# Expert gate weights: one-hot products on TensorE replaced by 384 adding indirect DMAs into a zeroed DRAM table, and 40 tiles of gelu results kept on chip

## What is computed

```
sc = scores of 8 heads x 2 halves against 128 keys each
s_top, i_top = top_k(sc, 16)                       # per half
best, pos = top_k(all 16 x 16 sums, 16)            # per head
idx = i_top[half 0] * 128 + i_top[half 1]          # 16384 experts
g = softmax(best)
out = sum over 8 heads x 16 ranks of  g * gelu(u_tab[idx] . x) * v_tab[idx]
```

## Time and profile before

| | |
|---|---|
| median of 3 runs | 2199.63 us (2199.42 to 2200.46) |
| span of the profiled execution | 2200.7 us, so about 1 us over the median |
| PE, DVE, ACT, POOL busy | 95%, 77%, 38%, 35% of the span |
| DMA, mean over the span | 195 GB/s |
| u stage | 1087 to 1662 us of the span |
| v stage | 1662 to 2187 us of the span |

### The profile page before, as it was taken

The page is one execution under the profiler, slowest core; times in us unless marked ns, Lnnn a source line. Parts: engine busy times, 40 slices in busy tenths (PEclk is TensorE's granted clock), DMA queues, the critical chain, the costliest instruction groups (busy, mean ns, idle before and its releaser), DMA issues.

```text
span 2200.7 us, 35703 instructions
## 1 busy us (share of the span) xinstructions
PE 2099.8 (95%) x11175; PEld 1853.1 (84%) x11175; DVE 1692.5 (77%) x3372; ACT 828.2 (38%) x1439; POOL 773.6 (35%) x672
## 2 busy tenths in 40 slices
PE   6998988979999998999899999999999999999997
PEld 4886788758888877899899999999998888888886
DVE  3776555677778744999688888888877888888887
ACT  4454423522323224244444444444433333333333
POOL 2000044500000000334478988988743222222221
PEclk9999989989999999999999999999999999999999
DMA  6743100405234224124477988988789999999995
GB/s 136 94 59 39 20 1 20 133 14 138 69 96 111 79 82 158 58 80 142 165 245 255 320 292 285 315 284 298 256 297 343 342 335 339 338 338 338 336 340 197
DMA packets 229811, 428.46 MB, mean 195 GB/s; under 512 B 18500, under 2 KB 155876, under 8 KB 229476
## 3 DMA queue, kind: packets, MB, share of 16 engines
q1 hardware_dynamic: 173108, 255.96, 38.5%
q0 software_dynamic: 41472, 151.01, 19.9%
q10 hardware_dynamic: 15152, 20.51, 2.6%
HBM read 381.28 MB, written 46.14 MB: 194 GB/s over the span
## 4 chain that ended last, share of the span: by engine, by line
PE 48%; DMA 1%; DVE 1%; POOL 0%; issue 0%; SPq 0%; ACT 0%; DVEq 0%; POOLq 0%
PE bank L2222 22%; PE bank L2205 20%; PE bank L2186 4%; PE bank L2194 2%; DMA v_gg<-weights 1%; DMA acts<-u_weight_lo 0%; POOL row_slot L1957 0%; DVE u_spread L2380 0%; DVE v_residual L2370 0%; POOL u_two L2128 0%; DVE u_lo L2339 0%; DVEq L2051 0%; SPq L2066 0%; ACT u_spread L2471 0%; SPq L2062 0%
## 5 line engine op out<-in xcount | busy, mean ns | idle before, releaser
L2222 PE MATMUL bank<-u_hi,u_one 128*128 128x512 f32 x768 | 299.1, 389 | 1.6 <-DVE u_two L2342 1.5
L2222 PE MATMUL bank<-u_lo,u_one 128*128 128x512 f32 x768 | 298.8, 389 | 0.0
L2222 PE MATMUL bank<-u_hi,u_two 128*128 128x512 f32 x768 | 298.8, 389 | 0.0
L2205 PE MATMUL bank<-xt_hi,u_hi 128*128 128x384 f32 x832 | 287.1, 345 | 0.0
L2205 PE MATMUL bank<-xt_hi,u_lo 128*128 128x384 f32 x832 | 279.0, 335 | 0.0
L2205 PE MATMUL bank<-xt_lo,u_hi 128*128 128x384 f32 x832 | 278.7, 335 | 0.0
L1957 POOL DMA_INDIRECT row_slot<-in_peer_v_dram,row_index x128 | 141.1, 1102 | 388.0 <-DVE row_x L2350 365.3
L2416 ACT ACTIVATE u_hi<-xh 128x1024 fp32r<-128x1024 f32 x128 | 135.9, 1061 | 330.4 <-PE bank L2222 329.8
L2339 DVE TENSOR_TENSOR u_lo<-xh,u_hi 128x1024 fp32r<-128x1024 f32 x128 | 156.8, 1225 | 78.8 <-ACT u_hi L2416 76.0
L1641 POOL TENSOR_TENSOR k_wlo<-q_raw,k_whi 128x2048 fp32r<-128x2048 f32 x4 | 18.7, 4683 | 467.0 <-ACT k_whi L1769 467.0
L2128 POOL TENSOR_TENSOR u_two<-u_match,u_weight_hi 128x512 fp32r<-128x512 f32 x96 | 162.3, 1691 | 50.7 <-DVE u_match L2268 49.7
(11 more groups left out here) (440 smaller groups left out, 4947.2 us busy)
## 6 DMA issues: line engine op xcount, KB each, us to landing
xh<-in_peer_v_dram SPq DMA_DIRECT2D x128, 512.0 KB
xh<-in_peer_u_dram SPq DMA_DIRECT2D x104, 512.0 KB, 4.5
x_raw<-in_w_in_dram SPq DMA_DIRECT2D x56, 512.0 KB, 6.9
v_ga<-acts SPq DMA_DIRECT2D x128, 192.0 KB
acts<-xh ACTq DMA_DIRECT2D x102, 192.0 KB
weights<-u_spread POOLq DMA_DIRECT2D x32, 512.0 KB
v_gg<-weights SPq DMA_DIRECT2D x128, 128.0 KB
p_raw<-in_w_in_dram SPq DMA_DIRECT2D x12, 1024.0 KB, 10.2
```

The source lines that it names most:

```text
L2205: mm = pe.matmul(k.ps[4 + b][:, 0:DENSE], w[b][:, c, :], x[:, c, 0:DENSE], start=(c == 0 and w is uhi and x is hi), stop=(c == DC - 1 and ...
L2222: mm = pe.matmul(k.ps[q][:, :], h[b][:, t * P:(t + 1) * P], w[b][:, f], start=start and h is hhi and w is vhi, stop=stop and h is hlo, ski ...
```

## The change

1. `delta_prepare` also writes the whole gate table (`weights`, 128 x 128 x 384 floats, 25.2 MB) with zeros: POOL clears a tile of 384 columns, SP issues 8 DMAs and waits for them before the stage's barrier.
2. In `choose_experts` the exp of the chosen scores, the softmax and the addresses are made step by step (`make_gates`, called a step later, after the ranks of the next step) instead of once at the end. `turn_chosen` and the copies to `chosen` go.
3. Each gate weight is added to its place in the table by an indirect DMA of POOL's queue with an adding write, 128 words of 4 bytes (one rank of one head for one tile of 128 tokens): 8 x 16 x 3 = 384 of them. 64 are issued in `choose_experts`, between POOL's low parts, the other 320 in the u stage, spread over tiles 1 to 98 of 104, in one queue with the row gathers. A scatter of head h waits for all 16 of head h - 1 for the same token tile.
4. The one-hots, `weigh`, `spread_tokens`, the sums into `u_spread` and the stores of the table go.
5. The gelu results of the last 40 tiles stay on chip (`kept_acts`, 60 KB per partition, in the place of `u_spread`); they are neither stored nor loaded. The weights are loaded for all 384 tokens (192 KB per tile, before 128 KB).
6. In the v stage DVE multiplies gelu by weight in one instruction right ahead of the tile's low parts, no longer one tile ahead. ACT's first `split` comes after the last gelu. DVE's u stage is unrolled, with 128 dots spread over 104 tiles.

```diff
@@ delta_prepare @@
+            @block.sync
+            def _(sp):
+                n = EXPERT_TILES // pieces
+                sp.wait_ge(zero_made, 1)
+                for i in range(pieces):
+                    sp.dma_start(zeroed[i * n:(i + 1) * n].rearrange("c p t -> p c t"), zero[:, :].unsqueeze(1).to_broadcast([P, n, DENSE])
+                                 ).then_inc(zeros_out, 16)
+                sp.wait_ge(zeros_out, 16 * pieces)
@@ choose_experts @@
-                    if e == EARLY - 1:
-                        turn_chosen()
...
-                    if e == EARLY - 6:
-                        act.wait_ge(s["shifted"], after(steps))
-                        act.activation(best[:, :, :, :], best[:, :, :, :], ACT.Exp).then_inc(s["exped"], 1)
+                    if e in exps_at:
+                        exp(exps_at[e])
...
+                scatters = 0
                 for e in range(EARLY):
                     pool.wait_ge(u_copied, after(4 * (e + 1)))
                     pool.tensor_tensor(u_lo[e % 4], u_turn[e % 2], u_hi[e % 4].bitcast(F32), ALU.subtract).then_inc(u_low, 1)
+                    if e == 2:
+                        pool.wait_ge(s["gate_made"], after(1))
+                    while scatters < EARLY_SCATTERS * (e - 1) // (EARLY - 2):
+                        scatter_weight(pool, table, gate, scatters, scattered)
+                        scatters += 1
...
+def scatter_weight(pool, table, gate, nth, scattered):
+    h, t, a = nth // (LAST * TOPK), nth // TOPK % LAST, nth % TOPK
+    r = h * TOPK + a
+    if h:
+        pool.wait_ge(scattered[t], 16 * TOPK * h)
+    pool.indirect_dma_start(table, bass.IndirectOffsetOnAxis(ap=gate["at"][:, t, r:r + 1], axis=0), gate["weight"][:, t, r:r + 1], None,
+                            compute_op=ALU.add).then_inc(scattered[t], 16)
@@ expert_products, POOL @@
-                pool.wait_ge(weight_split, after(3))
-                weigh(0)
-                fetched = SLOTS
-                for i in range(tiles):
-                    if i + 1 < steps:
-                        weigh(i + 1)
...
+                scatters, fetched = EARLY_SCATTERS, SLOTS
+                left = LAST * RANKS - EARLY_SCATTERS
+                for i in range(1, tiles + 1):
+                    while fetched < min(SLOTS + P * i // tiles, P):
                         fetch(fetched)
                         fetched += 1
+                    while scatters < min(EARLY_SCATTERS + left * i // (tiles - MARGIN), LAST * RANKS):
+                        scatter_weight(pool, table, gate, scatters, scattered)
+                        scatters += 1
@@ expert_products, PE @@
                         multiply(n, u)
-                        if c is not None:
-                            spread_tokens(n * PER + u, u % 2)
@@ expert_products, DVE @@
+                for n in range(rounds):
                     for u in range(PER):
                         if ahead(n, u):
                             low(n, u + 1)
+                        while dots < P * (n * PER + u + 1) // tiles:
+                            dot(dots)
+                            dots += 1
@@ expert_products, SP @@
+                for t in range(LAST):
+                    sp.wait_ge(scattered[t], 16 * RANKS)
+                for u in range(PER):
+                    load_weights(0, u)
@@ expert_products, ACT @@
-                        else:
-                            act.wait_ge(spread_ready, after(steps))
-                            split(0, 0)
...
+                with act.Fori(0, out_rounds) as n:
+                    stored(n)
+                with act.Fori(out_rounds, rounds - 1) as n:
+                    kept(n)
+                kept(rounds - 1)
                 act.wait_ge(dot_done, after(P))
                 act.activation(rows["dot"][:, :], rows["dot"][:, :], ACT.Gelu_apprx_tanh).then_inc(acted, 1)
-                for u in range(1, PER):
-                    split(0, u)
-                with act.Fori(1, v_rounds) as n:
+                with act.Fori(0, v_rounds) as n:
                     for u in range(PER):
                         split(n, u)
```

More of the change, by code:

```diff
@@ L1928, in _ @@
[L1928 to L1934, removed]
@@ L2270, in keep @@
-                def keep(c, step):
-                    for m in range(2):
-                        dve.wait_ge(high_kept, after(step * 2 + (m + 1)))
-                        to, parts = places(c, step, m)
-                        dve.tensor_tensor(to, to, parts[:, 1, :, :], ALU.add).then_inc(spread_kept, 1)
-                def dot(n, slot, count):
-                    dve.wait_ge(row_in[slot], count * 16)
-                    dve.scalar_tensor_tensor(out=rows["slots"][slot][:, :], in0=rows["slots"][slot][:, :], scalar=1.0, in1=rows["x"][:, :],
-                                             op0=ALU.mult, op1=ALU.mult, accum_out=rows["dot"][:, bass.ds(n, 1)]).then_inc(dot_done, 1)
@@ L2283, in body @@
-                def body(n, c):
-                    for u in range(PER):
-                        low(n, u + 1)
-                        if c is not None:
-                            step = n * PER + u
-                            dve.wait_ge(spread_ready, after(step))
-                            dve.wait_ge(two_done, after(step * 2 + 2))
-                            onehots(bass.ds(step * TOK_TILE + TOK_TILE, TOK_TILE), (u + 1) % 2)
-                            dot(n * SLOTS + u, u, n + 1)
-                            keep(c, step)
-                    dot(n * SLOTS + PER, PER, n + 1)
@@ L2296, in late_rounds, with dot @@
-                def late_rounds(n):
+                def dot(n):
+                    dve.wait_ge(row_in[n % SLOTS], (n // SLOTS + 1) * 16)
+                    slot = rows["slots"][n % SLOTS]
+                    dve.scalar_tensor_tensor(out=slot[:, :], in0=slot[:, :], scalar=1.0, in1=rows["x"][:, :],
+                                             op0=ALU.mult, op1=ALU.mult, accum_out=rows["dot"][:, n:n + 1]).then_inc(dot_done, 1)
+                low(0, 0)
+                dots = 0
+                for n in range(rounds):
@@ L2402, in high @@
                                        ACT.Copy).then_inc(s["hi_done"][b], 1)
-                def spread_high(c, step):
-                    act.wait_ge(spread_ready, after(step + 1))
-                    for m in range(2):
-                        to, parts = places(c, step, m)
-                        act.activation(to, parts[:, 0, :, :], ACT.Copy).then_inc(high_kept, 1)
                 def split(n, u):
```

344 lines of the change are left out of this document (134 added, 210 removed).

## The result

| | before | after |
|---|---|---|
| median of 4 runs each | 2199.81 us (2199.42 to 2200.46) | 2506.95 us (2505.43 to 2507.85) |
| ratio, 95% interval | | 1.139 (1.138 to 1.140) |
| span of the profiled execution | 2200.7 us | 2504.4 us |

The change costs 307 us. I had said 2303 us, slower; the direction and the place were right, the size was not: the time lies above my range. From barrier to barrier the stages differ thus: `delta_prepare` 100.4 us before, 97.7 after; `choose_experts` 243.6 and 300.1; `expert_products` 1113.4 and 1361.2; the others within 1.5 us. So 56.5 us come from the early tiles and 247.8 us from the expert stages.

A forecast was written before the change was run, and what follows sets the result against it. PE was taken to bound the u and v stages, with POOL becoming the u stage's bound after the change. Early tiles +17, u stage +83 and v stage +3 made +103 us, so 2303 us; range 2185 to 2500.

The forecast's parts named there:

- I take 1.24 us, the nearest row, because the number of addresses is the same: On POOL's queue, a scatter was priced from start to start like a gather, 0.94 us plus a 0.30 us gap.
- upper end, 1.71: Upper price in us of a scatter on POOL, if reading its target before writing adds half.
- The second rival: On POOL, an adding scatter is dearer because it fetches its target: at 1.71 us, 2482 us in all; chance 0.22.
- Stalls, 90 us: In the u stage, 128 dots on DVE would hold POOL's indirects for 0.7 us each, 90 us in all.
- The two rows that I set against each other: Two gathers before the change: one begun inside a dot took 1.81 us, one beside a one-hot 0.98 us.
- The rival without stalls: Dots leave POOL's indirects alone: +13 us, 2213 us; chance 0.13.
- Early tiles, +17 us: Among the early tiles, POOL's low parts and 61 scatters need 18 us more; transposes save 1 us.
- c: The price of a scatter on POOL from start to start; the change was to break even at 0.97 us.
- u stage, +83 us: POOL's 448 indirects and stalls become the bound of the u stage, about 6.2 us a tile: +83 us.
- v stage, +3 us: In the v stage, 88 tiles load more bytes through nearly full DMA engines: 0 to 6 us, taken as +3.
- zeros, 0: Writing 25.2 MB of zeros takes 70 us in a 100 us stage with no other DMA: no cost.
- The other side: Scatters on POOL's u-stage queue are cheap, at most 0.79 us, so PE's 44 us are won: 2162 us; chance 0.16.

The follow-up runs named there:

- experiment 1: The changed kernel with scatters that write their weights instead of adding them: 2282.6 us.
- experiment 4: The changed kernel with the dots of gathered rows reading their second factor from PSUM instead of SBUF, whatever stands there: 2459.8 us.
- experiment 2: The changed kernel without any of the 384 scatters, so the gate table stays zero: 2163.3 us.
- experiment 7: The changed kernel with row gathers that add to their buffers from the sixth on, and dots multiplied by zero: 2623.2 us.

## Why the prediction was wrong in size

- **The step that failed: "I take 1.24 us, the nearest row, because the number of addresses is the same".** A scatter takes 1.85 us from start to start. The reason was sound for a scatter that writes (0.954 + 0.305 = 1.26 us, experiment 1) and missed what the adding costs. I had put that in the upper end, 1.71, and 1.85 lies above that too.
- **The second rival** (a dearer scatter, 2482 us, chance 0.22) named the right cause, and should have been the forecast. Its working was wrong: a factor of 1.5 on POOL's descriptor work gives 1.41 us, measured 1.54. The Trainium skill, Collectives: The Full Stack, section The bandwidth ceiling: the fold count and why AG ≠ RS ≠ AR, says that the add of a collective needs two source descriptors for a chunk where a copy needs one, and nothing of an indirect DMA; the slopes of the table (2.2 ns for an added address, 1.0 ns for a written one, each between 64 and 128) are compatible with more descriptors, but most of the price doesn't go with the addresses. No run shows descriptors themselves. That the adding costs POOL more was right, and I gave it half the chance of the plain analogy.
- **Stalls, 90 us:** measured 46 (experiment 4). A dot does hold an indirect, by up to 1.1 us (2.63 against 1.54), but only one that starts in it, and for what is left of the dot less 0.12 us: 96 indirects for 128 dots, 0.46 us each, where I had counted nearly every dot with 0.7. The two rows that I set against each other don't contradict: the gather of 1.81 us began 0.27 us into a dot, and the one-hot began 0.01 us after the gather of 0.98 us. The rival without stalls is excluded: taking one SBUF input away took the stalls away.
- **The quoted inference.** I had said that the row of 1.81 us speaks against what the Trainium skill infers in SBUF — State Buffer, section Who interferes with whom, that a DVE instruction with two SBUF inputs leaves the writing of descriptors alone. It doesn't. The same section says that such an instruction contends with a POOL instruction that reads SBUF, and an indirect takes its addresses from columns in SBUF (`gate["at"]`, `rows["index"]`). The trace agrees with both: an indirect is held at its start, and dots that began 0.1 us or later, while it went on, held none of 87. That it is the reading of the addresses that waits is argued, not shown.
- **Early tiles, +17 us:** measured 56.5. The formula holds: 21 x 2.44 + 61 x 1.85 = 164 against 108.5, less 1 for the transposes, is 54.6. c was wrong; the formula also lacks the 3.3 us that the stage takes longer without any scatter (experiment 2).
- **u stage, +83 us:** from the first gather to the first v matmul 822 us, +247. With the measured terms: 320 x 1.85 = 592, 128 gathers of 1.31 us = 168, stalls 46, and 13.4 us from the last gather to PE (12 predicted), sum 819. The mechanism (DVE waits for rows, PE for DVE's low part) is in the waits above. That PE is busy for 77 to 81%, about the 80% that I had said, is luck: for a tile of 6.2 us PE's 5.06 us are 82%, for the measured 7.8 us they would be 65%. The clock of 0.86 to 0.91, which I hadn't counted, stretches PE's work (a matmul of L2167 takes 369 to 383 ns on average, those of L2205 before 335 to 345); whether that is all of the difference stays open.
- **v stage, +3 us; zeros, 0:** measured 0.4 and -2.7 us. Asking a share of 0.99 of the DMA cost nothing.
- **The other side** needed c of 0.97 us or less; even a writing scatter is at 1.26.

With c = 1.85 and stalls of 46 us my sum gives 381 x 1.85 - 369 - 44 = +292 us; measured +304 of span. Most of the rest of 12 us is the gathers' 1.31 us in place of 1.24 (9 us).

## What to carry to other kernels

Before work moves to a queue of indirect DMAs, count them, multiply by the time from start to start, and compare with the room that the queue has; its busy share hides the 0.3 us between them. An operation that differs from the nearest row in one property (here the adding) deserves a bound on that property from a run, not a factor on the part that one imagines. Where DVE runs beside POOL's indirects, look whether its instruction can take one input from PSUM; what counts is what DVE does when an indirect starts.

## What was not expected of the hardware

- Adding costs POOL 0.585 us for each indirect DMA of 128 addresses, the same (0.557) for gathers of 4096-byte rows; with 32 addresses an adding scatter still takes 1.31 us.
- An indirect that starts while DVE runs an instruction with two SBUF inputs is held until that ends (longer by the rest less 0.12 us, 96 indirects beside dots and 112 beside TENSOR_TENSORs); one that started 0.1 us or more before it isn't.
- An adding transfer of rows also costs the DMA engines: 300 GB/s at a share of 1.06 instead of 353 at 1.00 (experiment 7).
- The granted clock in the u stage fell to 0.86 to 0.91 while PE waited for part of each tile, and was 1.00 in the same loop without waits (experiment 2). POOL set the pace, so it cost nothing here.
